# Two orders changed around the output projection of a Mamba-2 / mixture-of-experts block: the second tile's products ahead of the first tile's transposes, and the routing of 13 tiles behind tile 14's norm

## The chip, the cores and the metric

The kernel runs on one core of one Trainium2 chip. The metric is the device time of one execution in microseconds (us); lower is better. Names of engines: PE is TensorE's matmuls, PEld its weight loads, DVE is VectorE, ACT is ScalarE, POOL is GpSimd and SP is SyncE, which here only issues transfers. PEq, ACTq and SPq are the engines' instruction queues.

## The reference, cut to what matters

One layer over 2048 tokens of width 1024: a Mamba-2 mixer, DeepNorm and layer norm, and a mixture of 32 experts in 4 groups, of which each token takes 2 in one group. The change is in the part between the mixer and the experts: the output projection, the norm and the router.

```python
y = y.astype(h.dtype) @ w_out                       # 2048 -> 1024, end of the mixer
x = layer_norm(ALPHA * x + (1 + g1) * y, ln_g[0], ln_b[0])
hm = x * (1 + sc2) + sh2
logits = hm @ w_router + b_router                   # 32 experts
probs = softmax(logits)
pg = probs.reshape(T, 4, 8)
group_score = sum(top_k(pg, 2)[0], -1)              # best group of experts
g_sel = argmax(group_score, -1)
top_p, top_local = top_k(pg[g_sel], 2)              # best two experts in it
gates = top_p / sum(top_p)
... # tokens sorted by expert, expert products, layer norm, out
```

## The kernel before, in words

The program has three stages one after the other: `mixer_steps` (which ends in `out_projection`), `experts` and `output`. A barrier and a clearing of semaphores stand between stages, so what `out_projection` loses at its end moves all that follows.

`out_projection` goes over 16 tiles of 128 tokens (TT = 16). Each engine runs its own queue in the order in which the code issues, and the engines meet only at semaphores. `loop` issues `step(i, b)` for i = 0 to 15, and for PE, ACT and DVE also for i = 16; steps 2 to 13 are a hardware loop of two steps a round, steps 0, 1, 14, 15 and 16 are issued by themselves. The work of one tile is spread over the queues:

- PE, step i: `products(b, 0)` and `products(b, 1)`, the two halves (512 columns each) of tile i's output projection, 48 matmuls of 512 columns each half (high x high, high x low, low x high parts; `op`, L1566). `turn(i - 1)` transposes the normed tile before (`h2`, shown as `h`) with 8 transposes into `tp` (L1579). `logits(i - 1)` multiplies the copied transpose `h2t` by the router's weights (`lgP`, L1591). The products of tile 0 are made earlier, among the mixer's last work, so that PE's step 0 is empty.
- DVE, step i: `tile(i - 1)`, the norm chain: two products with g1 (L1727), each behind its half of the projection, the sum with the residual `r` (L1731), the statistics (L1735 to L1742), then, behind ACT's L1662, the two operations that make `h2` (L1745, L1747). Then `low(i + 1)`, the low part of the mixer's output two tiles on (`ylo`, L1697), one operation for each half.
- ACT, step i: the normalising of `r` (L1662), the store of `h2` (L1666), two copies of the transposes to `h2t` (L1673), the store of `r` to `alpha_x` (L1678), and the high part of `y` two tiles on (`yhi`, L1651), one operation for each half.
- POOL makes the power for the norm (L1550) and multiplies and adds on `r` (L1554, L1556) ahead of its store.
- SP loads the residual rows `r` (L1529), each behind the store of `r` of the tile before (there is one buffer), and `yraw` (L1516), half by half, the second half of tile i + 1 behind the load of `r` of tile i.

The routing of tokens is `choose(r, t0, n)` on DVE: a chain of some 35 small operations, each waiting for the one before it. `choose(0, 0, 13)` treats tiles 0 to 12 at once, `choose(1, 13, 3)` the last three after the loop. It reads the logits of all its tiles, subtracts their largest value (third operation, which increments `p_ready`), waits for the exponential, which is `power(r, n)` on ACT, and goes on. `rank(0, 13)` on PE sums up the choices of the 13 tiles in `position` and `total`; it stands at the head of PE's step 16.

The logits of all tiles lie in one PSUM tensor, `lgP`, and `choose(0, ...)` reads it. From tile 13 on, `logits(j)` therefore waits before it writes there:

```python
if isinstance(j, int) and j >= EARLY:        # EARLY = 13
    pe.wait_ge(p_ready, 1)
```

PE's step 14 ends with `logits(13)`, and ACT waits for `lg_mm` at j ahead of its copies of tile j. In the kernel before, DVE's step 14 is `tile(13)`, `low(15)`, `choose(0, 0, 13)`, and its step 15 is `tile(14)`.

Of the kernel before, what the change touches and what calls it, by code (L numbers as in the profile page):

```python
# [17 lines left out]
TT = SEQ // P  # L18
# [26 lines left out]
EARLY = 13  # L45
# [5 lines left out]
def in_loop(i, low=0, high=1 << 30):  # L51

    return not isinstance(i, int) or low <= i < high
# [1416 lines left out]
def out_projection(nc, k, o, block, first, tail):  # L1470
# [24 lines left out]
    def loop(eng, step, extra=0):  # L1495
        step(0, 0)
        step(1, 1)
        with eng.Fori(1, TT // 2 - 1) as h:
            step(2 * h, 0)
            step(2 * h + 1, 1)  # L1500
        for i in range(TT - 2, TT + extra):
            step(i, i % 2)

    def probs(n):

        return flat[:, 0:n * E] if n == EARLY else flat[:, NE:NE + n * E]
# [53 lines left out]
    @block.tensor  # L1560
    def _(pe):
        def products(b, n):
            q = 0
            for yp, wp in ((yhi, w_hi), (yhi, w_lo), (ylo, w_hi)):
                for m in range(YTILES):
                    mm = nc.tensor.matmul(op[b][n][:], yp[b][m // HALF][:, m % HALF, :], wp[m][:, n * 512:(n + 1) * 512],  # L1566
                                          start=q == 0, stop=q == 3 * YTILES - 1)
                    q += 1
            mm.then_inc(o_mm, 1)

        def turn(j):
            pe.wait_ge(h2_done, j + 1)
            if in_loop(j, 1):
                pe.wait_ge(ht_done, 2 * j)
            else:
                pe.wait_ge(*tail.y_done)
            for n in range(2):
                for q in range(4):
                    tr = nc.tensor.transpose(tp[n][:, q * P:(q + 1) * P],  # L1579
                                             h2[:, (4 * n + q) * P:(4 * n + q + 1) * P], k.ident[:])  # L1580
                tr.then_inc(tr_done, 1)

        def logits(j):
            pe.wait_ge(ht_done, 2 * (j + 1))
            if not in_loop(j, 1):
                pe.wait_ge(wr_in, 16)
            if isinstance(j, int) and j >= EARLY:

                pe.wait_ge(p_ready, 1)
            for kk in range(KK):  # L1590
                mm = nc.tensor.matmul(lgP[:, bass.ds(j * EXPERTS, EXPERTS)], h2t[:, kk, :], wr[:, kk, :],  # L1591
                                      start=kk == 0, stop=kk == KK - 1)
            mm.then_inc(lg_mm, 1)

        def step(i, b):

            here, before = in_loop(i, 0, TT), in_loop(i, 1, TT + 1)
            if not in_loop(i, 1):
                return
            if not in_loop(i, 2):  # L1600

                pe.wait_ge(*tail.yt_out)
                pe.wait_ge(*tail.gm_done)
            if here:
                pe.wait_ge(lo_done, 2 * (i + 1))
                if in_loop(i, 2):

                    pe.wait_ge(t_done, 2 * (i - 1))
                products(b, 0)
            if isinstance(i, int) and i == TT:  # L1610
                rank(0, EARLY)
            final = isinstance(i, int) and i == TT - 1
            if before and not final:
                turn(i - 1)
            if here:
                products(b, 1)
            if final:
                turn(i - 1)
            if before:
                logits(i - 1)  # L1620

        def rank(t0, t1):

            pe.wait_ge(eq_ready, 1 if t0 == 0 else 2)
            if t0 == 0:
                pe.wait_ge(t_done, 2 * (TT - 1))
                nc.tensor.matmul(position[:], k.below[:], eq, start=True, stop=False, skip_group_check=True)
            else:
                nc.tensor.matmul(position[:, t0 * E:], k.below[:], eq[:, t0 * E:], start=False, stop=False,
                                 skip_group_check=True)  # L1630
            for t in range(t0, t1):
                part = eq[:, t * E:(t + 1) * E]
                if t + 1 < TT:
                    nc.tensor.matmul(position[:, (t + 1) * E:].rearrange("p (n e) -> p n e", e=E), k.ones[:],
                                     part.unsqueeze(1).to_broadcast([P, TT - 1 - t, E]), start=False,
                                     stop=t == TT - 2, skip_group_check=True)
                mm = nc.tensor.matmul(total[:, 0:E], k.ones[:], part, start=t == 0, stop=t == TT - 1,
                                      skip_group_check=True)
            mm.then_inc(pos_mm, 1)

        loop(pe, step, 1)
        rank(EARLY, TT)

    @block.scalar
    def _(act):
        def split_half(i, b, half):
            act.wait_ge(y_in, 16 * (2 * i + half + 1))
            if half == 0 and in_loop(i, 2):

                act.wait_ge(o_mm, 2 * (i - 1))  # L1650
            nc.scalar.copy(yhi[b][half][:], yraw[:]).then_inc(hi_done, 1)  # L1651

        def split(i, b):
            for half in range(2):
                split_half(i, b, half)

        def step(i, b):

            j = i - 1
            if in_loop(j, 0, TT):  # L1660
                act.wait_ge(nmr_done, j + 1)
                nc.scalar.activation(r[:], r[:], ACT.Identity, bias=nmr[:], scale=rstd[:]).then_inc(xn_done, 1)  # L1662
                act.wait_ge(h2_done, j + 1)
                if in_loop(j, 1, TT):
                    act.wait_ge(h2_out, 16 * j)
                act.dma_start(k.h2d[bass.ds(j * P, P), :], h2[:]).then_inc(h2_out, 16)  # L1666
                if in_loop(j, 1, TT):
                    act.wait_ge(lg_mm, j)
                if not in_loop(j, 1):
                    act.wait_ge(*tail.y_stored[1])  # L1670
                for n in range(2):
                    act.wait_ge(tr_done, 2 * j + n + 1)
                    nc.scalar.copy(h2t[:, 4 * n:4 * n + 4, :].rearrange("p q t -> p (q t)"), tp[n][:]  # L1673
                                   ).then_inc(ht_done, 1)
                if isinstance(j, int) and j == TT - 1:
                    power(1, TT - EARLY)
                act.wait_ge(xa_done, j + 1)
                act.dma_start(k.xad[bass.ds(j, 1)].rearrange("a p n -> (a p) n"), r[:]).then_inc(xa_out, 16)  # L1678
            if in_loop(i, 1, TT - 1):
                split(i + 1, 1 - b)  # L1680
            if isinstance(i, int) and i == TT - 2:
                power(0, EARLY)

        def power(r, n):
            act.wait_ge(p_ready, r + 1)
            p = probs(n)
            nc.scalar.activation(p, p, ACT.Exp).then_inc(exp_done, 1)

        loop(act, step, 1)
        act.wait_ge(xa_out, 16 * TT)  # L1690
        act.wait_ge(h2_out, 16 * TT)

    @block.vector
    def _(dve):
# [5 lines left out]
        def low(i, b):  # L1700
            for half in range(2):
                low_half(i, b, half)

        def mix_rows():

            for y in tail.y_stored:
                dve.wait_ge(*y)
            dve.wait_ge(*tail.ymm)
            dve.wait_ge(*tail.yn_tr)
            dve.wait_ge(row_in, 16 * 5)  # L1710
            nc.vector.tensor_tensor(mixed, k.a2[:], k.b1[:], ALU.mult).then_inc(mix, 1)
            dve.wait_ge(mix, 1)
            nc.vector.tensor_tensor(k.b2[:], k.b2[:], mixed, ALU.add).then_inc(mix, 1)
            nc.vector.tensor_tensor(k.a2[:], k.a2[:], k.a1[:], ALU.mult).then_inc(mix, 1)
            dve.wait_ge(mix, 3)
            for v in (k.a1, k.b1):
                nc.vector.tensor_scalar(v[:], v[:], ALPHA, None, ALU.mult).then_inc(mix, 1)
            dve.wait_ge(mix, 5)
# [30 lines left out]
        def step(i, b):  # L1749

            if in_loop(i, 1):
                tile(i - 1, 1 - b)
            if in_loop(i, 1, TT - 1):
                low(i + 1, 1 - b)
            if not in_loop(i, 1):
                mix_rows()
            if isinstance(i, int) and i == TT - 2:
                choose(0, 0, EARLY)

        count = [0]  # L1760
        v = nc.vector
# [30 lines left out]
        def choose(r, t0, n):  # L1792
# [35 lines left out]
            for g in (ga, gb):  # L1828
                link(v.tensor_tensor(g, g, s, ALU.mult))

        loop(dve, step, 1)
        choose(1, EARLY, TT - EARLY)
        dve.wait_ge(pos_mm, 2)
# [628 lines left out]
```

## Time and profile before

| what | us |
|---|---|
| median of 3 runs | 2989.3 |
| lowest and highest run | 2984.44 and 2990.38 |
| the profiled execution | 2990.43 |
| its span | 2988.6 |

The profiled execution's time is 1.8 us longer than the span between its first and last instruction. In the views, times are counted from the start of the span. `[11.69 <-DVE h L1747]` behind a line says that the engine was idle for 11.69 us before it and that this operation of DVE ended the wait. In a timeline, instructions of one kind are merged: the first number is the start, the second the time to the end of the last of them, and x8 their count.

### The profile page before, as it was taken

The page shows a single profiled execution, that of the slowest core. Times are in us where ns is not written, and L with a number is a line of the kernel's source. Part 1 is how long each engine was busy: PE and PEld are TensorE (multiplying, and loading weights), DVE is VectorE, ACT ScalarE, POOL GpSimd, SP SyncE. Part 2 cuts the span into 40 slices and gives each one's busy share as a digit, 9 for nine tenths or more (in the row PEclk, how much of TensorE's full clock was granted, in tenths as well). Part 3 has the DMA queues.
Part 4 walks back from the last instruction along what each step waited for, and adds up shares of the span by engine and source line. Part 5 has one row for each costly group of instructions (what it writes and reads, how often), then busy time and mean ns, then how long its engine had stood idle before and what let it go on. Part 6 is the DMA issues. An engine that isn't in the chain of part 4 may idle for free. (4 is left out here: it accounts for less than half of the span.)

```text
span 2988.6 us, 41030 instructions
## 1 busy us (share of the span) xinstructions
PE 2718.9 (91%) x14603; PEld 2316.1 (77%) x14603; DVE 2218.1 (74%) x2647; ACT 1315.9 (44%) x1655; POOL 1489.7 (50%) x755
## 2 busy tenths in 40 slices
PE   3899999999999999999979999949999999999920
PEld 2688888888889888888868888747888888888820
DVE  7678777777878777887863333458888888888857
ACT  4443333343433333343431111126777777777733
POOL 0133433343343334334432222126899999999963
PEclk9899999999999999999989999959999999999965
DMA  8844544444553544455252322249878869678676
GB/s 271 310 183 145 211 155 171 174 171 161 184 211 137 190 175 165 166 184 197 95 169 106 105 105 105 78 152 373 319 269 293 307 242 341 233 259 288 245 273 247
DMA packets 253185, 610.13 MB, mean 204 GB/s; under 512 B 15968, under 2 KB 98560, under 8 KB 244864
## 3 DMA queue, kind: packets, MB, share of 16 engines
q1 hardware_dynamic: 228208, 525.26, 49.2%
q0 software_dynamic: 11520, 41.95, 3.7%
q10 hardware_dynamic: 13328, 41.21, 3.4%
q8 instruction: 79, 1.29, 0.2%
q14 instruction: 50, 0.41, 0.0%
HBM read 600.75 MB, written 99.89 MB: 234 GB/s over the span
## 5 line engine op out<-in xcount | busy, mean ns | idle before, releaser
L1933 DVE TENSOR_TENSOR piece_lo<-piece_raw,piece_hi 128x2048 fp32r<-128x2048 f32 x187 | 563.3, 3031 | 102.5 <-ACT piece_hi L2040 101.3
L2040 ACT CAST piece_hi<-piece_raw 128x2048 fp32r<-128x2048 f32 x280 | 526.7, 1910 | 217.8 <-issue 77.8
L1933 POOL TENSOR_TENSOR piece_lo<-piece_raw,piece_hi 128x2048 fp32r<-128x2048 f32 x93 | 558.9, 6010 | 34.5 <-ACT piece_hi L2040 32.3
L574 PE MATMUL op<-hm,w_hi 128*128 128x512 f32 x2048 | 533.4, 406 | 45.2 <-DVE hm L1236 45.2
L1110 DVE SCALAR_TENSOR_TENSOR cv<-ub,par,cv 128x512 f32<-128x512 f32 x384 | 381.0, 992 | 157.1 <-ACT cv L833 147.9
L574 PEld LDWEIGHTS op<-hm,w_hi 128*128 128x128 f32 x2048 | 379.8, 190 | 119.5 <-DVE hm L1236 45.2
L524 POOL TENSOR_TENSOR xw<-xw,t 128x512 f32<-128x512 f32 x64 | 98.7, 1543 | 488.6 <-DVE t L1178 488.5
L589 PE MATMUL pz<-wz_hi,hm 128*128 128x256 f32 x2048 | 296.9, 290 | 1.1 <-DVE wz_lo L1088 0.5
L589 PEld LDWEIGHTS pz<-wz_hi,hm 128*128 128x128 f32 x2048 | 266.8, 192 | 7.4 <-DVE wz_lo L1088 3.9
L574 PE MATMUL op<-hm,w_lo 128*128 128x512 f32 x1024 | 254.9, 391 | 0.0
L505 POOL TENSOR_TENSOR xdt<-xw,tab 128x512 f32<-128x512 f32 x64 | 70.4, 1100 | 369.3 <-ACT xw L852 345.1
L574 PEld LDWEIGHTS op<-hm,w_lo 128*128 128x128 f32 x1024 | 192.4, 188 | 42.9
L1983 PE MATMUL gp_e<-piece_lo,xt_hi 128*128 128x512 f32 x368 | 151.7, 412 | 4.1 <-DVE xt_lo L2093 4.1
L1983 PE MATMUL yp<-piece_lo,ht_hi 128*128 128x512 f32 x368 | 150.0, 407 | 6.0 <-DVE ht_lo L2128 6.0
L1945 POOL DMA_INDIRECT xg<-hm,ix x48 | 127.7, 2660 | 39.0 <-POOL ix L1942 39.0
L1983 PE MATMUL gp_e<-piece_hi,xt_hi 128*128 128x512 f32 x368 | 146.8, 399 | 0.0
L1983 PE MATMUL gp_e<-piece_hi,xt_lo 128*128 128x512 f32 x368 | 146.5, 398 | 0.0
L1983 PE MATMUL yp<-piece_hi,ht_lo 128*128 128x512 f32 x368 | 146.1, 397 | 0.0
L1983 PE MATMUL yp<-piece_hi,ht_hi 128*128 128x512 f32 x368 | 145.9, 397 | 0.0
L1983 PE MATMUL up_e<-piece_lo,xt_hi 128*128 128x512 f32 x368 | 145.5, 395 | 0.0
L1983 PE MATMUL up_e<-piece_hi,xt_hi 128*128 128x512 f32 x368 | 145.5, 395 | 0.0
L1550 POOL TENSOR_TENSOR rstd<-ve,negh 128x1 f32<-128x1 f32 x16 | 8.8, 550 | 274.2 <-DVE ve L1740 274.2
(338 smaller groups left out, 5698.2 us busy)
## 6 DMA issues: line engine op xcount, KB each, us to landing
hm<-hm_parts SPq DMA_DIRECT2D x30, 4096.0 KB, 13.9
piece_raw<-in_w_gate SPq DMA_DIRECT2D x94, 1024.0 KB
piece_raw<-in_w_up SPq DMA_DIRECT2D x94, 1024.0 KB
piece_raw<-in_w_down SPq DMA_DIRECT2D x92, 1024.0 KB
decay<-acum_rows SPq DMA_DIRECT2D x32, 1024.0 KB
w_raw<-in_w_in SPq DMA_DIRECT2D x48, 512.0 KB, 7.5
expert_out<-ye ACTq DMA_DIRECT2D x46, 512.0 KB
w_ada_part<-in_w_ada_t SPq DMA_DIRECT2D x32, 512.0 KB, 3.9
```

The costliest lines, as they stand in the source:

```text
L505: nc.gpsimd.tensor_tensor(heads(xdt, h), heads(xw, h), k.tab[:, 0, part].unsqueeze(2).to_broadcast([P, 2 * RH, HD]), ALU.mult).then_inc(xd ...
L524: nc.gpsimd.tensor_tensor(x, x, t1[h][:], ALU.add).then_inc(y3, 1)
L574: mm = nc.tensor.matmul(pj[m % 2][:], wp[m][:, kk, :], hm[b][:, hp, kk, :], start=q == 0, stop=q == 3 * KK - 1)
L589: mm = nc.tensor.matmul(pz[:, (a % 2) * GW:(a % 2 + 1) * GW], hm[b][:, hp, kk, a * P:(a + 1) * P], wp[:, kk, :], start=q == 0, stop=q == 3 ...
L1110: nc.vector.scalar_tensor_tensor(out=cv[m % 2][:], in0=ub[:, m, t:t + SPAN], scalar=par[:, t:t + 1], in1=cv[m % 2][:], op0=ALU.mult, op1=A ...
L1550: nc.gpsimd.tensor_tensor(rstd[:], ve[:], k.negh[:, 0:1], ALU.pow).then_inc(rstd_done, 1)
L1933: v.tensor_tensor(lo[q][:], raw[q][:], hi[q][:].bitcast(F32), ALU.subtract).then_inc(lo_done[q], 1)
L1945: nc.gpsimd.indirect_dma_start(out=xg[b][:], out_offset=None, in_=k.h2d[:], in_offset=bass.IndirectOffsetOnAxis(ap=ix[b][:], axis=0)).then ...
L1983: mm = nc.tensor.matmul(acc[:], l[:, first + kk, :], r[:, kk, :], start=start and kk == 0 and n == 0, stop=stop and kk == 3 and n == 2)
L2040: nc.scalar.copy(hi[q][:], raw[q][:]).then_inc(hi_done[q], 1)
```

## The change

Three edits, all in the order of work:

1. PE, step 1: `turn(0)` stands behind `products(1, 1)` and no longer between the two halves. Step 15 had this order already.
2. DVE: `choose(0, 0, 13)` moves from the end of step 14, where it stood ahead of `tile(14)`, to step 15 behind `tile(14)`.
3. ACT: `power(0, 13)` moves from the end of step 14 into step 15. There it stands behind the store of tile 14's `h2` and the wait for `lg_mm`, and ahead of the copies of tile 14's transposes.

```diff
-            final = isinstance(i, int) and i == TT - 1
-            if before and not final:
+            behind = isinstance(i, int) and i in (1, TT - 1)
+            if before and not behind:
                 turn(i - 1)
             if here:
                 products(b, 1)
-            if final:
+            if behind:
                 turn(i - 1)
             if before:
                 logits(i - 1)
...
                 act.dma_start(k.h2d[bass.ds(j * P, P), :], h2[:]).then_inc(h2_out, 16)
                 if in_loop(j, 1, TT):
                     act.wait_ge(lg_mm, j)
+                if isinstance(j, int) and j == TT - 2:
+                    power(0, EARLY)
                 if not in_loop(j, 1):
                     act.wait_ge(*tail.y_stored[1])
                 for n in range(2):
...
             if in_loop(i, 1, TT - 1):
                 split(i + 1, 1 - b)
-            if isinstance(i, int) and i == TT - 2:
-                power(0, EARLY)
...
             if in_loop(i, 1):
                 tile(i - 1, 1 - b)
+            if isinstance(i, int) and i == TT - 1:
+                choose(0, 0, EARLY)
             if in_loop(i, 1, TT - 1):
                 low(i + 1, 1 - b)
             if not in_loop(i, 1):
                 mix_rows()
-            if isinstance(i, int) and i == TT - 2:
-                choose(0, 0, EARLY)
```

## Rows read from the trace of the kernel before

**Rows 1.** The page's first line.

```profile
span 2988.6 us, 41030 instructions
```

**Rows 2.** PE's waits, 1540 to 1970 us: sum, times, longest.

```profile
PE tp L1579 <- DVE h L1747: 14.4, 2, 11.7
PE lgP L1591 <- DVE yraw L1807: 0.8, 1, 0.8
```

**Rows 3.** Timeline of step 1: start, length, engine, line, operation.

```profile
1551.74 2.03 PE L1566 MATMUL op<-wo_hi,ylo1b 128*128 128x512 f32 x8
...
1565.46 1.97 PE L1579 MATMUL tp<-ident,h 128*128 128x128 f32 x8 [11.69 <-DVE h L1747]
...
1577.99 1.05 ACT L1651 CAST yhi0b<-yraw 128x1024 fp32r<-128x1024 f32 x1 [6.40 <-DMA yraw<-y_t]
...
1579.07 1.23 DVE L1697 TENSOR_TENSOR ylo0b<-yraw,yhi0b 128x1024 fp32r<-128x1024 f32 x1 [6.23 <-ACT yhi0b L1651]
...
1581.98 2.09 PE L1566 MATMUL op<-wo_hi,yhi0a 128*128 128x512 f32 x8
```

**Rows 4.** Timeline of step 2's end and the start of step 3.

```profile
1593.16 1.03 PE L1579 MATMUL tp<-ident,h 128*128 128x128 f32 x8
1593.96 2.09 PE L1566 MATMUL op<-wo_hi,yhi0a 128*128 128x512 f32 x8
...
1605.07 1.23 DVE L1697 TENSOR_TENSOR ylo1b<-yraw,yhi1b 128x1024 fp32r<-128x1024 f32 x1 [7.82 <-ACT yhi1b L1651]
1605.13 1.87 PE L1591 MATMUL lgP<-w_router,h2t 128*128 128x32 f32 x16
...
1606.83 0.48 PE L1566 MATMUL op<-wo_hi,yhi1a 128*128 128x512 f32 x1
```

**Rows 5.** Stretches: length, busy time by engine, granted clock (PEclk), DMA share, GB/s.

```profile
core 0: us, PE busy (x) PEld busy (x) DVE busy (x) ACT busy (x) POOL busy (x), PEclk, DMA share, GB/s
1557.70:1565.40 7.70, 0.00 (x0) 0.00 (x0) 5.48 (x8) 1.24 (x1) 1.66 (x2) 0.50 0.00 0
1565.40:1571.40 6.00, 5.94 (x18) 5.08 (x19) 0.00 (x1) 2.03 (x3) 4.59 (x2) 0.50 0.29 119
1946.80:1954.30 7.50, 5.58 (x24) 5.06 (x24) 1.20 (x1) 1.17 (x2) 5.67 (x2) 0.50 0.17 70
...
1532.10:1537.10 5.00, 4.96 (x14) 4.10 (x15) 4.83 (x6) 1.93 (x3) 0.00 (x0) 0.50 0.52 161
```

**Rows 6.** Timeline of tile 13's norm, tile 14's products and the routing.

```profile
1879.90 0.69 DVE L1727 TENSOR_TENSOR h<-op,g 128x512 f32<-128x512 f32 x1 [0.67 <-PE op L1566]
...
1887.20 1.22 DVE L1747 TENSOR_TENSOR h<-h,wo_raw 128x1024 f32<-128x1024 f32 x1
...
1902.72 2.01 PE L1566 MATMUL op<-wo_hi,ylo0b 128*128 128x512 f32 x8
1903.57 0.59 DVE L1805 TENSOR_TENSOR yraw<-lgP,rb 128x416 f32<-128x416 f32 x1
...
1905.56 1.94 PE L1591 MATMUL lgP<-w_router,h2t 128*128 128x32 f32 x16 [0.83 <-DVE yraw L1807]
...
1920.24 0.17 DVE L1829 TENSOR_TENSOR gate_b<-gate_b,sm 128x13 f32<-128x13 f32 x1
```

**Rows 7.** Timeline from tile 14's transposes to tile 15's logits.

```profile
1929.77 1.03 PE L1579 MATMUL tp<-ident,h 128*128 128x128 f32 x8
...
1931.59 2.21 PE L1591 MATMUL lgP<-w_router,h2t 128*128 128x32 f32 x16 [0.78 <-ACT h2t L1673]
1931.86 2.35 POOL L1556 TENSOR_TENSOR r<-r,wo_raw 128x1024 f32<-128x1024 f32 x1
...
1934.24 0.34 ACTq L1678 DMA_DIRECT2D alpha_x<-r  x1
...
1940.27 1.23 DVE L1731 SCALAR_TENSOR_TENSOR r<-r,h 128x1024 f32<-128x1024 f32 x1 [6.72 <-DMA r<-in_x]
...
1945.04 0.33 PE L1637 MATMUL op<-yraw,ones 128*128 128x32 f32 x2
...
1948.05 1.97 PE L1579 MATMUL tp<-ident,h 128*128 128x128 f32 x8 [2.68 <-DVE h L1747]
...
1950.69 3.62 PE L1591 MATMUL lgP<-w_router,h2t 128*128 128x32 f32 x16 [0.68 <-ACT h2t L1673]
```

## The prediction, made before the changed kernel was run

> **What bounds the kernel now.** I read the page's first line for the span (2988.6 us, [rows 1]), then the list of PE's waits over the output projection. The reader is to see how short that list is: the transposes wait 14.4 us in two places, 11.7 of it in one, and the logits wait 0.8 us once for the routing's third operation [rows 2]. Between 1582 and 1904 us the list is empty. So from step 2 to step 14 PE is the bound, and whatever PE loses or wins there goes to the end, as long as its inputs arrive.
>
> Next the timeline of step 1 and of step 2 [rows 3, 4]. PE ends the first half of tile 1's products at 1551.74 + 2.03 = 1553.77, waits for tile 0's norm, and transposes at 1565.46. This is the 11.7 us wait that edit 1 is about. The same rows show what comes next: tile 2's low part, which its products need, ends at 1579.07 + 1.23 = 1580.30, and PE gets to those products at 1581.98. The low part is only 1.7 us ahead of PE.
>
> Then the granted clock [rows 5]: 0.50 (the 1.2 GHz level) in the wait, and still 0.50 for 6.0 us after PE starts again; after another wait the stretch 1532.10 to 1537.10 has 0.50 for 5.0 us. Last the timeline of steps 13 to 16 [rows 6, 7], for who releases whom there.
>
> **Edit 1, transposes behind the second half.** Nothing is added or removed. A half of the products at full clock takes 1605.13 - 1593.96 = 11.17 us, the transposes 0.8 us (1593.16 to 1593.96), the logits 1.7 us (1605.13 to 1606.83) [rows 4]. The second half fills the wait: 1553.77 + 11.2 is 1565.0, just before tile 0's norm is ready. Transposes stay at 1565.46, the logits wait for ACT's copies as tile 14's do (1931.59 - 1929.77 = 1.8 us behind the transposes' start, [rows 7]) and end near 1569.0.
>
> What is late next: tile 2's first half, for its low part. That part hangs on the transfer of yraw [rows 3], which hangs in SP's queue on the load of r for tile 1, and this on the store of r of tile 0: nothing there hangs on PE's second half or on the transposes being early. I leave it at 1580.30. PE is thus idle for about 11.3 us again, only at another place, and starts at 1580.35, which is 1.6 us earlier than 1581.98. DVE starts tile 1's norm behind the same low part in both kernels.
>
> Does the wait cost clock as before? Before, from 1565.46 to 1581.98 PE took 16.52 us for work that costs 0.8 + 11.17 + 1.7 = 13.67: the cold start cost 2.85 us, and it lay before the 1580.30 limit, so that most of it was covered. Now the cold start lies behind the limit and nothing covers it. Half of 5.0 to 6.0 us of half clock [rows 5] is 2.5 to 2.95 us. Edit 1 is worth -1.63 + 2.5 to 2.95, which is +0.9 to +1.3; I take **+1.1 us**. If there were no cold start, the gain is at most 0.5 us, because tile 3's low part ends at 1606.30 and PE starts on it at 1606.83 [rows 4]. So the bounds are -0.5 and +1.3. I take the value near the upper end since a wait of the same length, 11.69 us, has the low clock in this trace.
>
> The Trainium skill, page "TensorE: Matmul & The Clock Gate", section "Part 1: The HAM clock gate", says that half rate is the default and activity releases the clock. By that rule edit 1 loses 1.1 us, without it it wins 0.5 us; the 0.50 behind the wait agrees with the rule.
>
> **Edits 2 and 3, the routing behind tile 14's norm.** No operation is added. But the third operation of the routing raises p_ready, and PE's logits of tile 13 wait for it. They are the last work of PE's step 14, and all of tile 15's products are queued behind them. Step by step:
>
> - PE ends tile 14's products at 1902.72 + 2.01 = 1904.73 [rows 6]. The norm of tile 14 can start its second multiplication there. In tile 13 it is 1887.20 + 1.22 - 1879.90 = 8.52 us from that multiplication to h2. So h2 of tile 14 is ready near 1913.3.
> - From the routing's first operation to PE's logits it is 1905.56 - 1903.57 = 1.99 us. So the logits of tile 13 start at 1915.3, where they started at 1905.56: **+9.75 us**, and the wait of 0.8 us becomes one of 10.5 us.
> - A wait of this length leaves the clock low again: 2.5 to 2.95 us, I take **+2.75**. Tile 14's transposes come at 1929.77 + 12.5 = 1942.3 [rows 7].
> - The routing's rest starts after ACT's exponential, which in ACT's queue waits for these logits (1915.3 + 3.6 at the low clock, as for tile 15 in [rows 7], is 1918.9). It takes 1920.41 - 1905.45 = 15 us [rows 6] and ends at 1934, hidden under tile 15's products, which end at 1942.3. Before, it lay ahead of tile 14's norm, and that norm (h2 at about 1929.6) was still in time for the transposes. Moving it frees little.
> - What does win: ACT's store of r of tile 14. Before, it waited until 1934.24 for POOL (1931.86 + 2.35), 2.65 us after ACT's copies were done (1931.59, when the logits start) [rows 7]. Now POOL is long done, and the store goes right behind the copies, at 1931.59 + 12.5 = 1944.1. That is +9.85 against 1934.24: **-2.65** of the 12.5.
> - Behind the store hang the load of r for tile 15, DVE's sum at 1940.27 (it waits 6.72 us for that load), and tile 15's transposes at 1948.05. They go to 1957.9. PE's ranking of the 13 tiles ended at 1945.04 + 0.33 = 1945.37 and goes to 1957.9 with the 12.5. Both arrive together, so neither adds.
> - Tile 15's transposes and logits ran at the low clock before (0.50 from 1946.80, [rows 5]): 1.97 for 1.03 us and 3.62 for 1.9 us. PE now comes to them straight from the ranking without the 2.7 us of idle time. That can give back nothing, or the whole 0.7 + 1.7 = 2.4 us. I take half, **-1.2**, since the rows hold neither case.
>
> Sum of edits 2 and 3: 9.75 + 2.75 - 2.65 - 1.2 = +8.65 us, bounds +7.2 and +10.1. With edit 1: **+9.75 us**. Nothing behind takes it up: the last three tiles' routing, the barrier and the experts' first loads all follow tile 15's logits. Against the profiled execution's own 2990.43 this is 3000.2; that execution is 1.1 us above the median of 2989.3, and the median plus 9.75 is 2999.05. I predict 2999.4.
>
> **The rivals.**
>
> *No cold starts.* Both waits occur, but the clock is back at once, or never falls. Then edit 1 is -0.5, and edits 2 and 3 are 9.75 - 2.65 - 2.4 = +4.7: together +4.2, 2993.5. Against it speak two waits in [rows 5], both followed by 0.50. Chance 0.07.
>
> *The ranking gets the bill.* PE's ranking ends with tile 15's norm to within 0.1 us in my sum. If the ranking is longer at its new place, cold or fed later, each microsecond goes to the end. Priced at 3 us more, which is about the low clock over half of its length, and with no warm logits behind it (+1.2), the sum is +14, 3003.3. For it: the ranking is made of short matmuls. Against: the products just ahead of it are dense, as before. Chance 0.08.
>
> *The first wait really goes.* This is the rival on the other side: tile 2's low part is ready when PE comes, near 1569.0, because the yraw transfer and its two operations move up. Then PE starts tile 2 at 1569.0 where it was 1581.98, -13.0 us at full clock, and with +8.65 the sum is -4.35, 2985.0, faster but by less than 0.2%. It decides only if the low part comes more than 8.7 us before 1580.3. Against it: ACT waits 6.40 us for the transfer [rows 3], and no store or load ahead of it is touched. Chance 0.03.
>
> *The order does not bite.* p_ready would have to rise before tile 14's norm, or the logits of tile 13 not wait for it. Then PE wins the 0.8 us wait and the store of r another 2.65, with edit 1 it is -2.4, 2986.9. The code's wait, and the 0.83 us that it already costs in [rows 6], speak against it. Chance 0.02.
>
> **How the numbers follow.** The forecast has 0.80. Its own sum runs from 7.2 - 0.5 = +6.7 to 10.1 + 1.3 = +11.4, 2996 to 3001; the three runs of before differ by 6 us among themselves. With half of the rivals on either side the range is 2993 to 3004. A difference of 0.2%, 6 us, is about what a measurement of this kernel can tell from none. Slower by over 0.2%: 0.80 and 0.08 from the ranking, 0.88. Within: 0.07 and most of the two small rivals, 0.10. Faster: 0.02.
>
> **What the profile after would show.** PE's list of waits: the transposes' 11.7 us gone, a new wait of about 11 us of PE for the low part (L1697) near 1569 to 1580, and one of about 10.5 us for the routing's third operation (L1807) in place of 0.8. Granted clock 0.50 behind both. Tile 1's transposes 1 us later, tile 14's near 1943, the store of r directly behind ACT's copies. I am wrong in edit 1 if the low part comes earlier, and in edits 2 and 3 if tile 13's logits start before 1913.

## The result, and the profile after

| | median us | runs | lowest to highest |
|---|---|---|---|
| before | 2986.3 | 6 | 2984.4 to 2990.4 |
| changed | 2998.8 | 6 | 2995.9 to 3001.9 |

The ratio is 1.004, with a 95% interval of 1.0027 to 1.0053: slower, by 8 to 16 us. The forecast was 2999.4, and slower by over 0.2% with 0.88. In the experiments below, one execution of e7 took 7083 us and one of the kernel before 5596 us; the ratios leave these two out. The profiled execution of the changed kernel took 2999.0 us with a span of 2997.3, 8.6 us more than that of before.

PE's waits, 1540 to 1990 us, in the changed kernel:

```profile
PE lgP L1591 <- DVE yraw L1807: 11.3, 1, 11.3
PE op L1566 <- DVE ylo0b L1697: 10.6, 1, 10.6
...
PE tp L1579 <- DVE h L1747: 1.9, 2, 1.3
```

Against [rows 2]: the 11.7 us of the transposes are gone, 10.6 us for the low part of tile 2 stand in their place, and the logits' wait for the routing has grown from 0.8 to 11.3 us.

To see where each microsecond lies I count from the first norm operation of tile 0 (L1727), which starts at 1556.31 before and at 1555.35 after; what comes before it is not touched by the change.

| from tile 0's first L1727 to | before | after | moved by | my sum had |
|---|---|---|---|---|
| tile 1's transposes | 36.85 | 36.63 | -0.2 | +1.1 |
| tile 13's logits | 349.25 | 359.55 | +10.3 | +10.85 |
| tile 14's transposes | 373.46 | 388.06 | +14.6 | +13.6 |
| the store of r of tile 14 | 377.93 | 389.14 | +11.2 | +10.95 |
| tile 15's transposes | 391.74 | 403.20 | +11.5 | +10.95 |
| the routing of the last three tiles | 398.04 | 407.52 | +9.5 | +9.75 |
| the first operation of the experts' stage | 418.74 | 428.21 | +9.5 | +9.75 |

The last line is the length of this part of the program; below I call it the stage's length. It shows small effects better than the whole execution, whose runs spread over 5 us and more. But it comes from one trace of each kernel, and one stretch of the same code differs between two traces by up to 1.4 us (see e2). What comes ahead of the stage and is never touched differs too: tile 0's first L1727 starts between 1550.35 and 1558.26 in the eleven traces.

**Step 1 and 2 after** (timeline, all of it in the order of time; to be held against [rows 3]):

```profile
1561.83 2.01 PE L1566 MATMUL op<-wo_hi,ylo1b 128*128 128x512 f32 x8
...
1564.51 1.09 PE L1579 MATMUL tp<-ident,h 128*128 128x128 f32 x8 [0.67 <-DVE h L1747]
...
1569.11 0.34 ACTq L1680 DMA_DIRECT2D alpha_x<-r  x1
1569.55 1.04 ACT L1651 CAST yhi0a<-yraw 128x1024 fp32r<-128x1024 f32 x1 [3.23 <-POOL r L1556]
1570.63 1.22 DVE L1697 TENSOR_TENSOR ylo0a<-yraw,yhi0a 128x1024 fp32r<-128x1024 f32 x1 [6.18 <-ACT yhi0a L1651]
1571.72 0.33 SPq L1529 DMA_DIRECT2D r<-in_x  x1
...
1577.61 1.23 DVE L1697 TENSOR_TENSOR ylo0b<-yraw,yhi0b 128x1024 fp32r<-128x1024 f32 x1 [5.75 <-ACT yhi0b L1651]
...
1578.98 3.78 PE L1566 MATMUL op<-wo_hi,yhi0a 128*128 128x512 f32 x8 [10.62 <-DVE ylo0b L1697]
```

PE has all 48 products of the half done before tile 0's norm is ready, and the transposes wait 0.67 us. Then it is idle until the low part. The chain that sets this is readable from below: low part behind high part (ACT) behind the transfer of yraw, and ahead of these the store of r (ACTq) and the load of r (SPq) in the queues. The first eight products then take 3.78 us, where they take 2.09 us at full clock.

**Steps 14 and 15 after** (timeline; against [rows 6, 7]):

```profile
1903.59 0.69 DVE L1727 TENSOR_TENSOR h<-op,g 128x512 f32<-128x512 f32 x1 [0.62 <-PE op L1566]
...
1910.88 1.23 DVE L1747 TENSOR_TENSOR h<-h,wo_raw 128x1024 f32<-128x1024 f32 x1
1910.99 3.32 POOL L1554 TENSOR_TENSOR r<-r,wo_raw 128x1024 f32<-128x1024 f32 x1 [2.87 <-DVE h L1745]
1912.02 0.58 DVE L1805 TENSOR_TENSOR yraw<-lgP,rb 128x416 f32<-128x416 f32 x1
...
1912.64 0.59 DVE L1806 TENSOR_REDUCE mx<-yraw 128x13 f32<-128x416 f32 x1
1913.26 1.49 DVE L1807 TENSOR_TENSOR yraw<-yraw,mx 128x416 f32<-128x416 f32 x1
...
1914.90 3.59 PE L1591 MATMUL lgP<-w_router,h2t 128*128 128x32 f32 x16 [11.35 <-DVE yraw L1807]
1918.31 3.76 PE L1566 MATMUL op<-wo_hi,yhi1a 128*128 128x512 f32 x8
...
1943.41 1.03 PE L1579 MATMUL tp<-ident,h 128*128 128x128 f32 x8
...
1944.49 0.34 ACTq L1680 DMA_DIRECT2D alpha_x<-r  x1
...
1950.78 1.23 DVE L1731 SCALAR_TENSOR_TENSOR r<-r,h 128x1024 f32<-128x1024 f32 x1 [4.95 <-DMA r<-in_x]
```

The norm of tile 14, 8.52 us from the second multiplication to h2, and behind it three routing operations, are now in front of PE. The granted clock by stretches:

```profile
1908.00:1914.90 6.90, 0.00 (x0) 0.03 (x1) 5.19 (x6) 1.24 (x1) 3.95 (x3) 0.50 0.19 76
1914.90:1920.00 5.10, 5.10 (x20) 4.81 (x21) 0.83 (x2) 0.55 (x1) 2.07 (x1) 0.50 0.01 3
1920.00:1923.00 3.00, 3.00 (x8) 2.32 (x8) 2.85 (x5) 0.00 (x0) 0.00 (x0) 0.50 0.00 0
1923.00:1925.00 2.00, 2.00 (x7) 1.57 (x7) 1.86 (x5) 0.00 (x0) 0.00 (x0) 0.69 0.00 0
1925.00:1928.00 3.00, 3.00 (x14) 2.42 (x13) 2.79 (x7) 0.00 (x0) 0.00 (x0) 1.00 0.00 0
```

It is 0.50 for 8.1 us after PE starts again, and 0.69 in the next 2 us stands for another 1.2 us of it: 9.3 us, longer than the 5 and 6 us of [rows 5]. From tile 13's logits to tile 14's transposes it is 28.5 us, against 1929.77 - 1905.56 = 24.2 before: the cold start cost 4.3 us.

### The profile page after: what moved, and what is told of

The parts are those of the page before. It is cut to its first block and busy times, and to the rows that moved or that the text cites. A ratio compares the mean times of both kernels' runs of the same rounds, so it can differ in the third digit from the quotient of the medians.

```text
span 2997.3 us, 41030 instructions
## 1 busy us (share of the span) xinstructions
PE 2716.8 (91%) x14603; PEld 2314.6 (77%) x14603; DVE 2218.6 (74%) x2647; ACT 1315.6 (44%) x1655; POOL 1493.0 (50%) x755
```

## The experiments

Stage lengths of all kernels, from one trace each, with the ratios of their times (each against runs of the kernel before on the same chip):

| kernel | stage, us | ratio to before | 95% interval |
|---|---|---|---|
| before | 418.7 | | |
| changed | 428.2 | 1.004 | 1.0027 to 1.0053 |
| e1, edit 1 alone | 419.2 | 1.0001 | 0.9992 to 1.001 |
| e2, edits 2 and 3 alone | 426.4 | 1.0028 | 1.0019 to 1.0037 |
| e3, head of the routing early | 413.3 | 0.999 | 0.9981 to 0.9999 |
| e4, waits filled | 425.7 | 1.0027 | 1.0018 to 1.0036 |
| e6, tile 13's logits late | 413.3 | 0.9982 | 0.9973 to 0.9991 |
| e7, edit 1 and yraw early | 412.8 | 0.9983 | 0.9973 to 0.9992 |
| e8, e3 and e7 | 412.0 | 0.9969 | 0.9958 to 0.9979 |
| e9, e8 in every step | 404.3 | 0.9943 | 0.993 to 0.9956 |
| e10, POOL's operation cut | 428.0 | one run | |

### e1: edit 1 alone

```diff
-            final = isinstance(i, int) and i == TT - 1
+            behind = isinstance(i, int) and i in (1, TT - 1)
```

> Edit 1 alone: the kernel before with tile 0's transposes behind both halves of tile 1's products; the routing stays where it was. Theory (the idle time only moves, to the wait for tile 2's low part, and costs the clock again there): within 1.5 us of the kernel before on either side, PE waits about 10.6 us for L1697 in place of 11.7 us for L1747, granted clock 0.50 behind it, and tile 1's transposes, counted from tile 0's first norm operation (L1727), come 36.6 us later (36.85 before). Rival 1, the wait really goes: about 11 us less than before. Rival 2, as my prediction had it: 1.1 us more than before.

Measured: 2989.4 us where the kernel before took 2990.0 beside it. The wait is 9.6 us for L1697 (10.6 expected; tile 0's logits, at a low clock, took 3.26 us, and 1.97 in the changed kernel), and tile 1's transposes come at 37.18 (36.6 expected, 36.85 before). Rival 1 falls: the wait does not go away. Rival 2, my own +1.1, is not excluded: the interval of the ratio is -2.4 to +3.0 us, and the stage is 0.4 us longer. The edit moves the idle time and changes nothing that can be measured.

### e2: edits 2 and 3 alone

PE's order in step 1 is that of before; `choose(0, 0, EARLY)` and `power(0, EARLY)` stand as in the changed kernel.

> Edits 2 and 3 alone: step 1 as before, the routing of 13 tiles and its exponential as in the changed kernel. Theory: the whole loss is here, 9 to 12 us more than before (ratio 1.003 to 1.004), with the wait of PE for L1807 at 11 us and tile 14's transposes some 14.5 us later. Rival: edit 1 carries a part of the loss; then this kernel is 1 to 3 us faster than the changed one and e1 slower than before by the same.

Measured: 2998.0 us against 2990.0, stage +7.7 us. The wait for L1807 is 11.3 us, tile 13's logits again take 3.59 us, and from them to tile 14's transposes it is 28.2 us. The loss of 8.0 us is most of that of the changed kernel, and the two intervals overlap. Both numbers are 1 to 1.3 us under the 9 to 12 that I expected: in this execution the cold start in step 1 cost 1.4 us less than in the kernel before, with the same code up to there (tile 1's transposes at 35.44, not 36.85). So most of the loss, if not all, is in edits 2 and 3. The rival is not quite refuted. This stage is 1.8 us shorter than the changed kernel's, of which 1.2 us lie ahead of tile 1's transposes, and as the cold start there differs by 1.4 us between two traces of the same code, one trace of each kernel can't say whether a microsecond of it belongs to edit 1.

### e3: the first three operations of the routing at their old place

```diff
+            if isinstance(i, int) and i == TT - 2:
+                choose(0, 0, EARLY, 1)        # to p_ready, ahead of tile(14)
...
             if isinstance(i, int) and i == TT - 1:
-                choose(0, 0, EARLY)
+                choose(0, 0, EARLY, 2)        # the rest, behind tile(14)
```

`power(0, EARLY)` is again at the end of ACT's step 14.

> The changed kernel, but the first three operations of the routing (up to the one that raises p_ready) and the exponential stand at their old places, at the end of step 14; the other operations stay behind tile 14's norm. Theory (only the late p_ready costs, by way of tile 13's logits): PE's wait for L1807 falls back to 0.8 us, tile 14's transposes come as in the kernel before, the store of r of tile 14 goes 2 to 3 us earlier, tile 15's transposes too, and the logits of tile 15 run at full clock: 2 to 6 us less than before, 12 to 18 less than the changed kernel. Rival 1 (the long rest of the routing behind tile 14's norm costs as well, as it stands ahead of tile 15's norm): 5 us or more above that, so at or above the kernel before. Rival 2 (the loss is not in this place): as the changed kernel.

Measured: 2986.9 us against 2990.0 (an interval of -0.3 to -5.7 us), stage -5.4 us against before and -14.9 against the changed kernel. Timeline from tile 14's transposes:

```profile
1926.26 1.03 PE L1579 MATMUL tp<-ident,h 128*128 128x128 f32 x8
1927.34 0.34 ACTq L1678 DMA_DIRECT2D alpha_x<-r  x1
1928.08 1.97 PE L1591 MATMUL lgP<-w_router,h2t 128*128 128x32 f32 x16 [0.78 <-ACT h2t L1673]
...
1933.74 1.22 DVE L1731 SCALAR_TENSOR_TENSOR r<-r,h 128x1024 f32<-128x1024 f32 x1 [4.44 <-DMA r<-in_x]
...
1941.51 1.09 PE L1579 MATMUL tp<-ident,h 128*128 128x128 f32 x8 [1.33 <-DVE h L1747]
1943.38 1.97 PE L1591 MATMUL lgP<-w_router,h2t 128*128 128x32 f32 x16 [0.78 <-ACT h2t L1673]
```

PE waits 0.8 us for the routing, tile 14's transposes come at 373.5, as before. The store of r follows them by 1.1 us, where [rows 7] have 4.5, and tile 15's logits run in 1.97 us, where [rows 7] have 3.62. The long rest of the routing behind tile 14's norm costs nothing. So three operations, 1.9 us of DVE work, and the exponential behind them decide whether this move loses 9.5 us or wins 5.4 of the stage.

### e4: both waits filled with matmuls

```diff
+        def warm(n):
+            for q in range(n):
+                w = w_hi[q % YTILES]
+                nc.tensor.matmul(cand[:], w[:, 0:P], w[:, 0:512], start=True, stop=True)
...
+            if isinstance(i, int) and i == TT - 2:
+                warm(44)
             if before:
                 logits(i - 1)
+            if isinstance(i, int) and i == 1:
+                warm(44)
```

> The changed kernel with 44 more matmuls of 512 columns, on the projection's weights and into a PSUM tensor that is free then, in each of the two waits: behind tile 0's logits and ahead of tile 13's. They take about 10.3 us in waits of 10.6 and 11.3 us; the outputs are not touched. Theory (each wait costs its length and then a cold start of 1.8 us at step 2 and 4.3 us at step 14): granted clock 1.00 behind both waits, tile 13's logits and tile 15's products at 24.2 us for 28.5, the whole 4 to 6 us below the changed kernel. Rival (the slow stretch is not the clock but supply of the operands or something after a wait): no gain, or a loss of up to 1 us for what the matmuls are longer than the waits.

Measured: 2996.5 us against 2990.0, ratio 1.0027 where the changed kernel has 1.004. The intervals overlap, so that the times alone do not show a gain; the stage is 2.5 us shorter than the changed kernel's, where I expected 4 to 6. In step 14 it is as the theory has it:

```profile
1905.75 10.35 PE L1574 MATMUL cand<-wo_hi 128*128 128x512 f32 x44
1917.30 1.94 PE L1596 MATMUL lgP<-w_router,h2t 128*128 128x32 f32 x16 [1.21 <-DVE yraw L1816]
...
1941.52 1.03 PE L1584 MATMUL tp<-ident,h 128*128 128x128 f32 x8
```

The logits take 1.94 us instead of 3.59, and to tile 14's transposes it is 24.2 us instead of 28.5. That is the cold start, 4.3 us, taken away by work alone. In step 1 the theory of the expectation fell short:

```profile
1568.06 2.49 PE L1596 MATMUL lgP<-w_router,h2t 128*128 128x32 f32 x16 [0.78 <-ACT h2t L1684]
1570.36 13.05 PE L1574 MATMUL cand<-wo_hi 128*128 128x512 f32 x44
1583.25 1.99 PE L1566 MATMUL op<-wo_hi,yhi0a 128*128 128x512 f32 x8
```

The granted clock was 1.00 up to 1568.06, 0.78 under tile 0's logits (2.49 us instead of the 1.97 of the changed kernel) and 0.50 behind them, so the filling matmuls took 13.05 us and not 10.35, and tile 2 started 2.6 us later than in the changed kernel. What they saved afterwards did not make up for that (tile 1's transposes at 37.3, not 36.6). At the end tile 15's logits ran at 0.51 and took 3.62 us, 1.2 more than in the changed kernel; that is the rest of what is missing.

### e6: tile 13's logits behind a half of tile 15's products

```diff
                 products(b, 0)
+            if isinstance(i, int) and i == TT - 1:
+                logits(i - 2)
...
-            if before:
+            if before and not (isinstance(i, int) and i == TT - 2):
                 logits(i - 1)
...
+                if isinstance(j, int) and j == TT - 2:
+                    power(0, EARLY)
                 if in_loop(j, 1, TT):
                     act.wait_ge(lg_mm, j)
-                if isinstance(j, int) and j == TT - 2:
-                    power(0, EARLY)
```

> The changed kernel, with the whole routing still behind tile 14's norm, but tile 13's logits no longer ahead of tile 15's products: they stand between the two halves of these, and ACT's exponential ahead of its wait for lg_mm. So the wait for p_ready has 11.2 us of products in front of it. Theory (the loss comes from what is queued behind that wait, not from the routing's place): the wait for L1807 is gone or under 1 us, tile 14's transposes 0 to 1 us earlier than before, tile 15's chain 2 to 3 us earlier, the whole 2 to 6 us less than before, as e3. Rival (the routing as a block behind tile 14's norm is itself what costs, by holding up DVE or POOL): 5 us or more above e3.

Measured: 2985.6 us against 2990.3, stage 413.3, the same as e3. Timeline of tile 13's logits:

```profile
1910.81 2.03 PE L1566 MATMUL op<-wo_hi,ylo1b 128*128 128x512 f32 x8
1911.33 1.56 DVE L1809 TENSOR_TENSOR yraw<-yraw,mx 128x416 f32<-128x416 f32 x1
...
1913.03 1.94 PE L1591 MATMUL lgP<-w_router,h2t 128*128 128x32 f32 x16 [0.19 <-DVE yraw L1809]
```

p_ready is as late as in the changed kernel, and PE waits 0.19 us for it. So it is not the routing's place that costs, but that 22 us of products were queued behind the wait for it. The rival falls: the whole routing stands behind tile 14's norm here, and costs nothing against e3. e3 and e6 undo the loss from the two ends of one wait, and end at the same stage length.

### e7: edit 1, with tile 2's low part early

```diff
+            first = isinstance(i, int) and i == 1
+            if first:
+                load_y(i + 1, 1)              # SP: ahead of r of tile 1
...
+            if first:
+                split_half(2, 0, 0)           # ACT: ahead of tile 0's L1662
...
+                if first:
+                    split_half(2, 0, 1)       # ACT: ahead of the store of r
                 act.wait_ge(xa_done, j + 1)
...
+            if not in_loop(j, 1):
+                low_half(2, 0, 0)             # DVE: where tile(0) waits for ACT
             dve.wait_ge(xn_done, j + 1)
```

> Edit 1 alone, with tile 2's low part taken out of the queues that hold it: the second half of yraw is loaded ahead of tile 1's r, ACT makes the first high half ahead of tile 0's normalising and the second behind its copies, ahead of the store of r, and DVE makes the first low half inside tile 0's norm, where it waits for ACT. Theory (edit 1 gains nothing because this low part limits step 2): the low part is ready 13 to 16 us behind tile 0's first norm operation (24.7 before), PE's wait for it falls from 10 us to 0 to 3, the clock stays at 1.00, and tile 1's transposes come 8 to 11 us earlier: 6 to 10 us less than before in all. Rival 1 (tile 1's own chain, whose r still waits for the store of r of tile 0, takes over as the limit): tile 1's transposes wait 2 us or more for h2, gain 3 to 6 us. Rival 2 (the chip pays the gain back later in the loop, as the low part of tile 3 was only 0.5 us ahead of PE): tile 14's transposes no earlier than in e1, no gain.

Measured: 2986.1 us against 2990.3, stage -6.4 us against e1 and -5.9 against before; I had expected 6 to 10 us less than before, so the 4.2 of the times are a miss. Timeline:

```profile
1570.21 2.86 DVE L1705 TENSOR_TENSOR ylo0b<-yraw,yhi0b 128x1024 fp32r<-128x1024 f32 x1 [2.86 <-ACT yhi0b L1654]
...
1573.22 3.77 PE L1569 MATMUL op<-wo_hi,yhi0a 128*128 128x512 f32 x8 [1.22 <-DVE ylo0b L1705]
...
1600.32 1.22 DVE L1705 TENSOR_TENSOR ylo1b<-yraw,yhi1b 128x1024 fp32r<-128x1024 f32 x1 [6.58 <-ACT yhi1b L1654]
...
1601.60 3.42 PE L1569 MATMUL op<-wo_hi,yhi1a 128*128 128x512 f32 x8 [1.55 <-DVE ylo1b L1705]
```

PE's wait falls from 9.6 to 1.2 us and tile 1's transposes come 9.2 us earlier (27.95 for 37.18). So the low part was the limit that took edit 1's gain. Rival 1 had the size (3 to 6 us) but not the cause: PE's list has no wait of tile 1's transposes. Rival 2 is half right: at step 3 PE waits 1.55 us for the next low part and runs cold again, and tile 2's transposes are only 6.2 us earlier. The clock part of the theory is wrong: after a wait of 1.2 us the products still took 3.77 us. The clock had fallen ahead of that wait: it was 1.00 up to 1569.29, 0.70 from there to 1571.90, while tile 0's logits ran, and 0.50 behind.

### e8 and e9: both places mended

e8 is e3 and e7 together.

> e3 and e7 together: edit 1 with the low part of tile 2 early, and the routing behind tile 14's norm except for its first three operations and the exponential. Theory (the two places are independent): the sum of both gains, 8 to 14 us less than before (ratio 0.995 to 0.997), the fastest of all. Rival (one gain eats the other): no better than the better of e3 and e7.

Measured: 2981.4 us against 2990.3, 8.9 less, within the 8 to 14 expected. The profiled stage is 412.0 us, a gain of 6.8 where the two alone have 5.4 and 5.9. Three stretches at the low clock took about the rest. At step 3 PE waited 1.7 us and then ran 16 products at the low clock, so that tile 2's transposes came 1.6 us later than in e7 (57.50, 55.89). At tile 13's logits the clock fell although PE waited only 0.9 us: 1.00 up to 1901.79, 0.88 under the logits, 0.50 behind them up to 1906.00.

```profile
1901.79 2.20 PE L1594 MATMUL lgP<-w_router,h2t 128*128 128x32 f32 x16 [0.89 <-DVE yraw L1822]
1903.80 3.44 PE L1569 MATMUL op<-wo_hi,yhi1a 128*128 128x512 f32 x8
```

From these logits to tile 14's transposes it is 25.8 us, where e3 and e7 have 24.2. And tile 15's logits took 3.62 us, where e3 has 1.97.

e9 takes the same order into every step: SP loads the second half of yraw ahead of r, ACT makes the first high half ahead of the copies of the transposes.

> The kernel with both places mended (e8), and its order of the second half of yraw ahead of r, and of the first high half ahead of the copies of the transposes, in every step instead of step 1 alone. Theory (in e7 and e8 a part of the gain at step 2 was given back at step 3, where PE waited 1.6 us for tile 3's low part and then ran 16 matmuls at the low clock): no wait for a low part from step 3 on, tile 2's transposes 4 to 5 us earlier than in e8, 2 to 5 us less than e8 in all, 10 to 15 less than before. Rival 1 (r of the next tile, now loaded behind yraw, becomes late): waits of DVE for r, no gain over e8 or a loss. Rival 2 (the wait at step 3 has another cause): as e8.

Measured: 2973.7 us (2970.3 to 2978.1, 6 runs) against 2991.8, 18.1 less (an interval of 13 to 21), stage 404.3 us, 14.5 less than before and 7.7 less than e8, more than the 2 to 5 expected. PE's waits in the stage:

```profile
PE op L1629 <- DVE yraw L1838: 8.0, 1, 8.0
PE lgP L1591 <- ACT h2t L1678: 2.3, 3, 0.8
PE op L1566 <- DVE ylo0b L1704: 2.0, 1, 2.0
PE tp L1579 <- DVE h L1756: 0.8, 1, 0.8
```

No wait for a low part from step 3 on, and none for the routing of the 13 tiles. Both rivals fall: from step 2 to 13 DVE's waits for r are 5.0 us in all, 4.1 in e8. Only a half of the 7.7 us is what the theory named: tile 2's transposes come 3.8 us earlier than in e8 (53.68 for 57.50; 4 to 5 expected). Most of the rest lies where e8 had the low clock, at tile 13's and at tile 15's logits. It is faster than the kernel before and the changed one.

### e10: POOL's multiplication cut to 8 columns

The multiplication L1554 treats 8 of 1024 columns for tile 14, so that most of this tile's r is left unscaled.

> The changed kernel, in which POOL multiplies only 8 of 1024 columns of tile 14's r (L1554), so that POOL is done with it early; the output of tile 14 is left unscaled in the other columns. Theory (the routing's third operation took 1.49 us instead of 0.59 because it could not run beside POOL's multiplication): unless it meets POOL's addition instead, it takes 0.59 us, and the logits of tile 13 start 0.9 us earlier relative to tile 14's norm; if it meets the addition it is stretched to that one's end. Rival (it is slow at this place for another reason, such as its operands behind the norm): 1.5 us whatever POOL does.

Timeline:

```profile
1905.81 1.22 DVE L1748 TENSOR_TENSOR h<-h,wo_raw 128x1024 f32<-128x1024 f32 x1
1905.92 1.18 POOL L1555 TENSOR_TENSOR r<-r,wo_raw 128x8 f32<-128x8 f32 x1 [2.87 <-DVE h L1746]
...
1907.18 2.34 POOL L1557 TENSOR_TENSOR r<-r,wo_raw 128x1024 f32<-128x1024 f32 x1
1907.57 0.59 DVE L1807 TENSOR_REDUCE mx<-yraw 128x13 f32<-128x416 f32 x1
1908.19 1.78 DVE L1808 TENSOR_TENSOR yraw<-yraw,mx 128x416 f32<-128x416 f32 x1
```

The routing's third operation now meets POOL's addition, and ends 0.45 us behind its end (1909.97 and 1909.52). In the changed kernel it ended 0.44 us behind the end of POOL's multiplication (1914.75 and 1914.31). The stretch follows POOL's operation, wherever that ends; the rival, which had 1.5 us whatever POOL does, falls. In e2, e4 and e6 the same operation also ended 0.45 us behind POOL's multiplication. The time itself (2993.5, one run) tells nothing.

## Why the prediction was right, point by point

- **The mechanism of edits 2 and 3** is as stated: the third routing operation raises p_ready, tile 13's logits wait for it, all of tile 15's products are queued behind. e3 and e6 each take this one link away and the loss turns into a gain.
- **The wait**, 9.75 us in the sum, was 10.5 (10.3 and 0.2 of edit 1). The norm's 8.52 us came out to the hundredth. The 1.99 us from the first routing operation to the logits became 2.9, since L1807 took 1.49 us for 0.59 beside POOL. I had costed the routing's head by a row in which POOL was idle.
- **The cold start behind it** is the term that was mis-sized: +2.75 (2.5 to 2.95) in the sum, 4.3 measured (4.0 in e2, 4.1 in e10), and e4 shows the whole of it to be the clock. The step that failed is the use of 5.0 and 6.0 us of low clock [rows 5] as bounds (half of 6.0 is 3.0, a slip that does not matter here). Here PE starts with the logits and was at the low clock for 9.3 us.
- **The gain at the store of r**, -2.65, was -3.4 (14.6 less 11.2). I had put the store 1.8 us behind the start of the transposes, where the logits start; it went out 1.1 us behind it.
- **Tile 15 at full clock**, 0 to -2.4, taken as -1.2, was -2.0. The transposes took 1.09 us and the logits 2.42. (By the lengths that the prediction quotes from [rows 7] the transposes could give back 0.9 us and not 0.7.)
- **Edit 1** was put at +1.1 with bounds of -0.5 and +1.3. The trace has -0.2, and e1 +0.4 on the stage and no difference in the time. The mechanism (the idle time moves to L1697, the clock is paid again) holds; the size is uncertain because the cold start differs from run to run. In the five kernels with edit 1 and the old order of yraw (changed, e1, e3, e6, e10) tile 1's transposes come at 36.6 to 37.3, without the edit at 36.85 and 35.44. e7 shows the limit that I named to be the one.
- **The errors cancel**: 0.75 (wait) and 1.55 (cold start) were missing, and 1.3 (edit 1), 0.75 (store) and 0.8 (tile 15) too much in it, another 0.3 came between the store and tile 15's transposes, and the sum of +9.75 stands beside 9.5 on the stage. That these misses leave only 0.25 us is luck. So is how close 2999.4 lies to 2998.8: the medians differ by 12.5 us and not 9.75, and the median of before that the forecast was added to, 2989.3 of 3 runs, is 3.0 us above that of 6 runs. The runs spread by 6 us in either kernel; edits 2 and 3 alone make 8.0.
- **The rivals**: no cold starts is refuted by the 0.50 of the stretches above. The ranking did not get the bill: tile 15's transposes waited 1.27 us for the norm and not for it. The other two are refuted by the waits. (The 8.7 us in the rival on the first wait count from 1581.98, where PE starts; from the low part's 1580.3 it is 7.0.)

## What to carry to other kernels

Before moving a block of work in an in-order queue, find the semaphores that it raises in its first operations, and what is queued behind those who wait for them: here the three operations that others need early belong at the old place, and the thirty that nobody waits for can go. A long wait of the bounding engine whose filling gains nothing points to a second limit right behind it; follow that one back through the transfers and their queues before the order is changed. When the bounding engine waits, its price is the wait and the slow stretch after it, which here was up to 4.3 us more.

## What the runs showed of the hardware that I had not expected

- **DVE and POOL on SBUF.** In these traces DVE's tensor_tensor with both inputs in SBUF made almost no progress while a POOL tensor_tensor was running. It ended 0.44 us (L1807 beside L1554) and 0.45 us (in e10, beside the addition) after that one's end; alone it takes 0.59 us in all. The low half of e7 took 2.86 us for 1.22 and ended at 1573.07, with POOL's addition ending at 1572.00. It goes the other way too: POOL's 8 columns in e10 took 1.18 us, begun 0.11 us behind L1748 of DVE, and ended 0.07 us behind it. The routing's first operation (L1805, an input in PSUM) and its reduction (L1806) took their 0.58 and 0.59 us beside the same POOL operation. The Trainium skill, page "SBUF — State Buffer", section "Who interferes with whom", says just this: a DVE instruction with two SBUF inputs contends with POOL's reads through a shared port, and tensor_reduce on this chip never does. The trace agrees.
- **The clock falls under work too.** In e4 the logits of tile 0, behind dense products, tile 0's transposes and a 0.78 us wait, took 2.49 us (3.26 in e1, 1.97 in the changed kernel) at a clock that fell beneath them (0.78 in that stretch, 1.00 before, 0.50 behind). In e7 the products were cold after a wait of only 1.2 us, and the clock had fallen before it, under the same logits (0.70). In e8 it fell at tile 13's logits, behind dense products and a 0.9 us wait. The cold start of one and the same place cost between 1.4 us (e2) and 2.85 us (before). So a wait that is cut short does not by itself save the cold start.
